# Two transformer blocks on one core: the order of the last projection's heads, the row slots and a run of table copies

## The reference, cut to what matters

```python
def peer_layer(h, w_q, sub_keys, u_tab, v_tab):
    ...
    q = (hf @ w_q).reshape(T, PEER_HEADS, 2, PEER_DQ // 2)
    s = jnp.einsum('thpd,hpnd->thpn', q, sub_keys)
    sc, idx = lax.top_k(s, PEER_TOPK)
    ...
    top_sc, pos = lax.top_k(cand, PEER_TOPK)
    eidx = jnp.take_along_axis(cidx, pos, axis=-1)
    gate = jax.nn.softmax(top_sc.astype(jnp.float32), axis=-1).astype(h.dtype)
    ...
        act = jax.nn.gelu(jnp.einsum('thkd,td->thk', u_tab[eb], hb), approximate=False)
        return jnp.einsum('thk,thkd->td', gb * act, v_tab[eb])
...
        u2 = rms_norm_2(h, norm2_g[l]) * (1 + sc2) + sh2
        h = h + g2 * peer_layer(u2, peer_wq[l], peer_keys[l], peer_u[l], peer_v[l])
    return rms_norm_2(h, final_g)
```

## Time and profile before

| what | value |
|---|---|
| median of 3 runs | 1728.81 us (1722.48 to 1732.06) |
| profiled execution: time | 1722.41 us |
| profiled execution: span of the core | 1720.6 us |
| TensorE busy | 1523.9 us (89%) |
| VectorE busy | 1026.8 us (60%) |
| ScalarE busy | 533.0 us (31%) |
| GpSimd busy | 558.6 us (32%) |
| mean TensorE clock granted | 0.95 of full |
| chain that ended last | PE 67%, DMA 20%, DVE 8% |
| row fetches | 256, 268.45 MB |

### The profile page before, as it was taken

The page is one execution under the profiler, slowest core; times in us unless marked ns, Lnnn a source line. Parts: engine busy times, 40 slices in busy tenths (PEclk is TensorE's granted clock), DMA queues, the critical chain, the costliest instruction groups (busy, mean ns, idle before and its releaser), DMA issues.

```text
span 1720.6 us, 22658 instructions
## 1 busy us (share of the span) xinstructions
PE 1523.9 (89%) x8228; PEld 1161.9 (68%) x8228; DVE 1026.8 (60%) x2104; ACT 533.0 (31%) x1069; POOL 558.6 (32%) x361
## 2 busy tenths in 40 slices
PE   6999989999699999999999989878787778777876
PEld 6999988678599999998889988433333333333332
DVE  5554355655233325998984744657676766758555
ACT  4443353352244335443116421312121212121111
POOL 3555353000134432001001402454454544444540
PEclk9999999899799998999999999898999998899998
DMA  6666699819979997998975836799999999999994
GB/s 264 241 227 247 245 350 378 279 46 342 386 284 371 370 366 284 365 371 308 346 255 196 342 105 275 307 428 426 428 426 427 427 427 427 426 427 427 427 427 194
DMA packets 98724, 571.87 MB, mean 332 GB/s; under 512 B 10960, under 2 KB 11088, under 8 KB 48976
## 3 DMA queue, kind: packets, MB, share of 16 engines
q1 hardware_dynamic: 60624, 297.89, 47.3%
q0 software_dynamic: 36864, 268.45, 37.1%
q10 hardware_dynamic: 1152, 4.43, 0.7%
HBM read 569.68 MB, written 135.27 MB: 410 GB/s over the span
## 4 chain that ended last, share of the span: by engine, by line
PE 67%; DMA 20%; DVE 8%; issue 2%; ACT 2%; SPq 2%; POOL 0%; ACTq 0%; DVEq 0%; POOLq 0%
DMA arena<-pairs,eidx 16%; PE ps L2125 11%; PE ps L1612 9%; PE ps L1614 9%; PE ps L1613 9%; PE ps L1957 5%; PE ps L2090 3%; PE ps L1663 2%; PE ps L1665 2%; PE ps L1664 2%; DMA ring<-pairs,eidx 2%; PE ps L1974 2%; DVE arena L1530 2%; DMA ring<-in_stream 1%; PE ps L1627 1%
## 5 line engine op out<-in xcount | busy, mean ns | idle before, releaser
L2125 PE MATMUL ps<-arena 128*128 128x512 f32 x720 | 346.3, 636 | 85.3 <-ACT arena L997 85.2
L634 POOL TENSOR_TENSOR w_lo<-ring,w_hi 128x1024 fp32r<-128x1024 f32 x82 | 216.2, 2638 | 446.7 <-DVE w_lo L1059 366.3
L2125 PEld LDWEIGHTS ps<-arena 128*128 128x128 f32 x720 | 144.2, 204 | 285.5 <-issue 174.1
L1612 PE MATMUL ps<-u_hi,w_hi 128*128 128x256 f32 (+1 forms) x1056 | 305.1, 289 | 9.9 <-DVE u_lo L1028 9.9
L1614 PE MATMUL ps<-u_hi,w_lo 128*128 128x256 f32 (+1 forms) x1056 | 303.3, 287 | 0.0
L1613 PE MATMUL ps<-u_lo,w_hi 128*128 128x256 f32 (+1 forms) x1056 | 302.9, 287 | 0.0
L1530 DVE CUSTOM_DVE_ANT_0 arena<-arena 128x1024 f32<-128x1024 f32 x180 | 218.9, 1223 | 138.7 <-DMA arena<-pairs,eidx 138.7
L664 POOL DMA_INDIRECT arena<-pairs,eidx x180 | 213.4, 1185 | 254.8 <-PE ps L2125 202.4
L681 ACT ACTIVATE w_hi<-ring 128x1024 fp32r<-128x1024 f32 x188 | 197.9, 1056 | 191.5 <-PE ps L1665 77.5
L1612 PEld LDWEIGHTS ps<-u_hi,w_hi 128*128 128x128 f32 x1056 | 201.9, 191 | 12.6 <-issue 10.7
L1614 PEld LDWEIGHTS ps<-u_hi,w_lo 128*128 128x128 f32 x1056 | 202.2, 192 | 0.0
(11 more groups left out here) (301 smaller groups left out, 2461.0 us busy)
## 6 DMA issues: line engine op xcount, KB each, us to landing
ring<-in_stream SPq DMA_DIRECT2D x130, 1024.0 KB, 7.0
pairs<-in_peer_u SPq DMA_DIRECT2D x128, 512.0 KB, 7.6
pairs<-in_peer_v SPq DMA_DIRECT2D x128, 512.0 KB, 8.8
arena<-in_ada SPq DMA_DIRECT2D x32, 768.0 KB, 6.3
arena<-pairs,eidx POOLq DMA_INDIRECT x180, 17.9
ring<-pairs,eidx POOLq DMA_INDIRECT x76, 17.3
h<-in_x_t SPq DMA_DIRECT2D x1, 1088.0 KB, 7.8
arena<-in_keys ACTq DMA_DIRECT2D x1, 1024.0 KB, 7.0
```

What stands on the lines that cost most here:

```text
L634: pool.tensor_tensor(lo[:, half, :], ring[:, slot, e * HALF:(e + 1) * HALF], hi[:, half, :], ALU.subtract).then_inc(used if e else lo_done, 1)
L1612: pe.matmul(dst, hi[:, half, block], x[0][:, b, 0:w], start=(b == 0), stop=False)
L2125: mm = pe.matmul(ps[:, Y_BANKS[j // TOPK] + half, :], diag[:, n % DIAGS, :], slot_of(n)[:, D + half * 512:D + half * 512 + 512], start=(hd ...
```

## The change

It has four parts. (1) The ten blocks behind the `ada` loads move in front of them (BEFORE_ADA = 24). (2) The first head is projected, scored and copied tile by tile, in products of 128 columns. Only heads 1 to 4 follow it; head 5 is done on TensorE and ScalarE behind group 1, head 6 behind group 8, head 7 behind group 12, followed by the gain. (3) There are again 13 row slots, now eleven in the arena (the room of `h_tok` and `final_g`) and two in the ring, those of the pieces of heads 4 and 5. Rows 0 to 10 go to the arena, row 11 to the ring when head 4 is projected, rows 12 to 19 to the slots of rows 0 to 7, row 20 to the ring when head 5 is projected; then the order repeats with period 13. The sums of the two tiles lie in PSUM banks 0 to 3. (4) The last four rows are groups of one. Of the last tile's work, gain, residual and squares of tile 0 go between the dots of rows 248 to 250, and both scalings and stores come at the end. h is transposed to PSUM banks 4 to 7 between groups 44 to 50 and read from there; `final_g` is loaded by SP once the last head is chosen.

```diff
 ADA_W = 6 * D // ADA_Q
-ARENA_SLOTS = 9
-SLOTS = ARENA_SLOTS + RING
+ARENA_SLOTS = 11
+SLOTS = ARENA_SLOTS + 2
 HEAD_ROWS = TT * TOPK
 ROWS = HEADS * HEAD_ROWS
 GROUP = 4
+GROUPS = [slice(n, n + GROUP) for n in range(0, ROWS - GROUP, GROUP)] + [slice(n, n + 1) for n in range(ROWS - GROUP, ROWS)]
+RING_HEADS = [4, 5]
+LATER_HEADS = {1: 5, 8: 6, 12: 7}
 DIAGS = 8
 N_BLOCKS = NKEYS * NKEYS // P
 W_IN_BLOCKS = 7
 ADA_BLOCKS = 1
-BEFORE_ADA = 14
-AFTER_ADA = 10
-FINAL_STEPS = 5
+BEFORE_ADA = 24
...
 
         NORM_COLS = [slice(0, T), slice(0, T), xc, xc, xc]
 
-        Y_BANKS = [2, 4]
+        Y_BANKS = [0, 2]
+        RING_SLOTS = [(BASE["wq"] + hd) % RING for hd in RING_HEADS]
+        SLOT_AT = list(range(ARENA_SLOTS)) + [ARENA_SLOTS] + list(range(8)) + [ARENA_SLOTS + 1]
+        while len(SLOT_AT) < ROWS:
+            SLOT_AT.append(SLOT_AT[-SLOTS])
+        TURN = [SLOT_AT[:n].count(SLOT_AT[n]) for n in range(ROWS)]
 
         def slot_of(n):
 
-            at = n % SLOTS
-            return rows[:, at, :] if at < ARENA_SLOTS else ring[:, at - ARENA_SLOTS, :]
+            at = SLOT_AT[n]
+            return rows[:, at, :] if at < ARENA_SLOTS else ring[:, RING_SLOTS[at - ARENA_SLOTS], :]
 
         def landing(n):
-            return row_in[n % SLOTS], n // SLOTS * 16 + 16
+            return row_in[SLOT_AT[n]], TURN[n] * 16 + 16
+
+        def held_before(n):
+            return max(i for i in range(n) if SLOT_AT[i] == SLOT_AT[n])
+
+        def q_bank(hd):
+            return 6 if hd >= 6 else hd % 2 * 2
+
+        def q_pieces(hd):
+            return 2 * hd + 2 * TT
+
+        def score_pieces(hd):
+            return hd + TT
 
 
...
                     for n in range(ADA_BLOCKS):
                         pair_up(kt * (ADA_Q * ADA_BLOCKS) + (at + q * ADA_BLOCKS + n))
             at += (KT // 2 - 2) * ADA_Q * ADA_BLOCKS
-            for n in range(AFTER_ADA):
-                pair_up(at + n)
-            at += AFTER_ADA
             for part, end, each in (("ffn2", "z_gate", 1), ("z_gate", "w_b", 2), ("w_b", "wq", 1)):
                 load_pieces(BASE[part], BASE[end], at, each)
                 at += (BASE[end] - BASE[part]) * each
             assert at == N_BLOCKS
             load_pieces(BASE["wq"], N_PIECES)
+            sp.wait_ge(idx_done, score_pieces(HEADS - 1))
+            sp.dma_start(final_g, a["final_g"].rearrange("(o d) -> o d", o=1).broadcast_to([P, D])).then_inc(final_in, 16)
             for t in range(TT):
-                sp.wait_ge(fin_step, (t + 1) * FINAL_STEPS)
+                sp.wait_ge(fin_step, 3 * TT + 2 * (t + 1))
                 sp.dma_start(out[0, t * P:(t + 1) * P, :], acc[:, t, :]).then_inc(out_done, 16)
             sp.wait_ge(out_done, 16 * TT)
 
...
+                    pool.wait_ge(idx_done, score_pieces(hd) if hd else 1)
                 elif hd == 0 and j == TOPK:
                     pool.wait_ge(idx_done, TT)
-                if n == ARENA_SLOTS:
-                    pool.wait_ge(q_mm, 2 * HEADS)
-                if n >= SLOTS:
-                    pool.wait_ge(row_summed, n - SLOTS + 1)
+                if TURN[n]:
+                    pool.wait_ge(row_summed, held_before(n) + 1)
+                elif SLOT_AT[n] >= ARENA_SLOTS:
+                    pool.wait_ge(q_mm, q_pieces(RING_HEADS[SLOT_AT[n] - ARENA_SLOTS]))
                 pool.indirect_dma_start(slot_of(n), None, pairs, bass.IndirectOffsetOnAxis(ap=eidx[:, n:n + 1], axis=0)
                                         ).then_inc(landing(n)[0], 16)
 
...
+            def first_head(t):
+
+                c = slice(t * P, (t + 1) * P)
                 for e in range(2):
-                    act.wait_ge(q_mm, hd * 2 + e + 1)
+                    act.wait_ge(q_mm, t * 2 + e + 1)
+                    act.activation(qh[:, 0, e, c], ps[:, e, c], ACT.Copy).then_inc(q_ev, 1)
+                tok_copy(2 * t)
+                act.wait_ge(sc_mm, t + 1)
+                act.activation(scores[:, 0, t].rearrange("p e n -> p (e n)"), ps[:, 4, t * SEQ:(t + 1) * SEQ], ACT.Copy
+                               ).then_inc(sc_ev, 1)
+                tok_copy(2 * t + 1)
...
+            for t in range(TT):
+                first_head(t)
+            for hd in range(1, min(LATER_HEADS.values())):
+                head(hd)
+                if hd == 2:
+                    gate_exp(0)
...
+                if g in LATER_HEADS:
+                    head(LATER_HEADS[g])
+                if g == max(LATER_HEADS):
+                    act.wait_ge(gain_mm, 1)
+                    for half in range(2):
+                        act.activation(y_gain[:, half * 512:half * 512 + 512], ps[:, 6 + half, :], ACT.Copy).then_inc(tok_ev, 1)
+            mean_root(0)
             mean_root(1)
...
-            def finish(t):
+                    dve.wait_ge(diag_made, group.stop - HEAD_ROWS)
+                dve.tensor_tensor(wts[:, j:end], dots[:, j:end],
+                                  gate[:, hd % 2].rearrange("p t k -> p (t k)")[:, j:end], ALU.mult).then_inc(w_done, 1)
+
+            def gained(t):
 
                 dve.wait_ge(row_summed, ROWS - (TT - 1 - t) * TOPK)
+                if t == 0:
+                    dve.wait_ge(tok_ev, 6)
                 summed = ps[:, Y_BANKS[t]:Y_BANKS[t] + 2, :].rearrange("p b d -> p (b d)")
-                if t == 0:
-                    dve.wait_ge(tok_ev, 10)
-                    dve.wait_ge(final_in, 16)
                 then(dve.tensor_tensor(acc[:, t, :], summed, y_gain, ALU.mult), fin_step)
-                then(dve.tensor_tensor(acc[:, t, :], acc[:, t, :], h_tok[:, t, :], ALU.add), fin_step)
+
+            def added(t):
+
+                dve.wait_ge(tok_mm, 2 * TT + 2 * t + 2)
+                kept = ps[:, 4 + 2 * t:6 + 2 * t, :].rearrange("p b d -> p (b d)")
+                then(dve.tensor_tensor(acc[:, t, :], acc[:, t, :], kept, ALU.add), fin_step)
+
+            def squared(t):
 
                 then(dve.tensor_tensor_reduce(hf[:, t, :], acc[:, t, :], acc[:, t, :], 1.0, 0.0, ALU.mult, ALU.add,
                                               fin[:, 2 * t:2 * t + 1]), fin_step)
+
+            def scaled(t):
+
...
+                for n in range(group.start, group.stop):
+                    dot(n)
+                    if n == group.start and g:
                         weights(g - 1)
+                    if n == ROWS - 8:
+                        gained(0)
+                    if n == ROWS - 7:
+                        added(0)
+                    if n == ROWS - 6:
+                        squared(0)
...
+            weights(len(GROUPS) - 1)
+            gained(1)
+            added(1)
+            squared(1)
+            scaled(0)
+            scaled(1)
...
+            def residual_turn(n):
+
+                t, half = n // 2, n % 2
+                if n == 0:
+                    pe.wait_ge(sc_ev, score_pieces(HEADS - 1))
+                    pe.wait_ge(tok_ev, 6)
+                for i in range(4):
+                    mm = pe.transpose(ps[:, 4 + n, i * P:(i + 1) * P], h[:, half * 4 + i, X0 + t * P:X0 + (t + 1) * P], ident)
+                mm.then_inc(tok_mm, 1)
...
+            def first_head(t):
+
+                slot = BASE["wq"] % RING
+                c = slice(t * P, (t + 1) * P)
+                if t == 0:
+                    pe.wait_ge(landed[slot], BASE["wq"] // RING * 16 + 16)
+                for e in range(2):
+                    for b in range(KT):
+                        if t == 0 and e == 0:
+                            pe.wait_ge(u_done, 4 * KT + b + 1)
+                        mm = pe.matmul(ps[:, e, c], blk(slot, e * KT + b), u[:, b, c], start=(b == 0), stop=(b == KT - 1))
+                    mm.then_inc(q_mm, 1)
+                if t == TT - 1:
+                    pe.wait_ge(q_mm, q_pieces(0))
+                    pe.sem_inc(used, 1)
+                tok_turn(2 * t)
+                pe.wait_ge(q_ev, 2 * t + 2)
+                scores_with(0, t).then_inc(sc_mm, 1)
+                tok_turn(2 * t + 1)
...
+                if hd < HEADS - RING:
+                    pe.wait_ge(q_mm, q_pieces(hd))
                     pe.sem_inc(used, 1)
...
+            for t in range(TT):
+                first_head(t)
+            for hd in range(1, min(LATER_HEADS.values())):
+                head(hd)
+            for g in range(len(GROUPS)):
+                if g - 1 in LATER_HEADS:
+                    head(LATER_HEADS[g - 1])
+                    if g - 1 == max(LATER_HEADS):
+                        gain_turn()
+                weigh_rows(g)
+                if len(GROUPS) - 23 <= g < len(GROUPS) - 15 and g % 2 == 0:
+                    residual_turn((g - (len(GROUPS) - 23)) // 2)
```

## The result

The changed kernel takes 1699.71 us (median of 4 runs, 1696.46 to 1700.80), the kernel before 1728.38 (median of 4, 1722.48 to 1732.06): ratio 0.9836, 95% interval 0.981 to 0.986, 28.7 us less. Its profiled execution took 1700.73 us, span 1698.9.

What follows compares the result with a forecast made beforehand. The prediction took the row stage to end when its copies end, with TensorE's early head projections the bound from 1060 to 1095 us. Gains 17.5 + 13 + 0 = 30.5 from 1728.8 gave 1698.3 us, range 1714 down to 1683.

Steps and rivals of the forecast that it cites:

- The copies, 17.5: Second feed-forward's norm: moving ten blocks of pair copies lets its weight pieces go earlier, gaining 17.5 us (bounds 12 and 20).
- The cost of the copies in the attention: First two ada loads go out 32 us later but stay hidden: cost 0, at most a few us.
- the sum by the page: Same norm: without the pause TensorE's clock may stay up, so the gain would be some 20 us, not 17.5.
- The row stream, 13: Fetch of the 256 expert rows: earlier start gives 20.5, late heads lose 7; ends 13 us earlier (bounds 5 and 22).
- the late end: Row 25 lands at 1107 to 1111 instead of 1131.6; taking the later time gives 20.5 us earlier.
- 15 us of lateness: Heads 6 and 7 behind groups 8 and 12: 7.8 and 10.9 late, some 3.5 made up, together about 15 us.
- The place of the pause (row 65): Sign in the row stream: a pause of 4 to 7 us around row 65, none if the late heads cost nothing.
- Rival 1: Late heads eat the row stream's gain, leaving only 3 to 5 us; time 1707 us; chance 0.18.
- rival 2: Late heads cost nothing because the row slots absorb all; time 1691 us; chance 0.12.
- The end, 0: After the last row lands: TensorE ends 8.9 us later, tile scaling adds 1; together 0 (2 worse to 4 better).
- The copies running into the attention (3): Second feed-forward does not start earlier: something such as these copies takes the gain back; time 1716 us; chance 0.07.
- TensorE as the bound of the rows (4): Row stream: groups restarting at the low clock cost more than 9.82 us each, so the kernel is slower; chance 0.03.

Runs made afterwards that it cites:

- twelve single rows: The changed kernel with one-row groups for the last twelve rows in place of four: 1690.47 us, ratio 0.9762 to the kernel before.
- four profiles of unchanged order: Two more profiles of the kernel before (1727.11, 1737.63 us) and two of the changed kernel with the copies put back (1720.34, 1714.47 us).
- `after`: The changed kernel as first measured, with all four parts, against the kernel before: 1699.71 us, ratio 0.9836; its profiled execution took 1700.73 us.

## Why the prediction was right

**The copies, 17.5: right, with some luck in the number.** The mean gain at the norm in front of the expert layer is 17.0 (1014.3 - 997.3), and 19.8 in the time of the kernel with only the copies moved. The mechanism is as told: the norm of the second feed-forward follows the projection without a pause in all eight profiles with moved copies, and its sum is ready 68.3 us behind the third ada load in each, where the six others need 85.6 to 88.7. They are held by the landing of two pieces in a loaded queue, which varies; the profile of before had the shortest. So at this point the copies give 19.2 in the mean and not 17.5, and some 2 of it are lost on the way to the expert layer, at TensorE's clock, which the sum had not foreseen: the two nearly cancel. The first piece was issued at the predicted place (426.62 less the 4.0 of the attention is 422.6). The cost of the copies in the attention was taken as 0, and is 0 as far as the profiles can tell. Without the pause the norm's 16 matmuls take 3.69 at a granted clock of 1.00, where they took 5.58 at 0.66. The rule of the Trainium skill that was weighed beside this term (TensorE: Matmul & The Clock Gate, "What's actually happening": an idle array is throttled until activity releases it) agrees with that. But the norm's sum was ready at 448.3 to 448.6 in the four profiles whose attention was not late, 448.0 predicted, and not 2.5 earlier as the sum by the page had it.

**The row stream, 13: right, with two steps that cancel.** Row 0 is issued 22.8 us behind the norm where 25.6 were, the 3 predicted (at 1021.49 and not near 1012, since the norm itself was late in this pair). A head takes 8.59 us by the two rows named for it, not 8.55, which changes the sum by 0.1. From the norm, row 25's dot comes 22.7 us earlier (124.5 to 101.8, means over four and seven profiles), where 20.5 was taken as the late end. From row 25 to row 255 the changed kernel takes 580.0 and the kernel before 570.3: 9.7 lost to heads 6 and 7, where the prediction had 7 from an estimate of 15 us of lateness. The lateness was 10.0 + 12.95 less 5.5 that three groups made up, so 17.4; the heads took 19.8 and 22.75 for the 17.6 and 20.7 worked out. With the heads at 12 and 20 the loss is 3.2 (573.5), and with only one head behind group 1 it is 0.9. So their place is shown to matter; two things change with it, the choosing part in the groups behind group 8 and the distance between the heads (four groups or eight), and no run parts them. The place of the pause (row 65) was right. Rival 1 had the loss too large, and rival 2 (no cost) is refuted by the windows and by the moved heads.

**The end, 0: right, 0.8 gained** (0.6 in the first pair): TensorE ends 8.5 after the last dot starts, 8.9 predicted: its last eight rows start 5.5 before that dot and take 14.0 (the prediction's own terms, 14.4 less 7.6, give 6.8; the 2.1 up to its 8.9 stand in none of its rows). The span ends 9.8 behind TensorE where 8.7 were, the 1 us more of the tiles' last work. That the backlog comes from group 62, not from the last four rows, is shown by the twelve single rows.

**Rivals 3 and 4.** The copies running into the attention (3) was what the first pair of profiles seemed to say, and four profiles of unchanged order took it back. TensorE as the bound of the rows (4) does not happen: from 1208 on the stream never pauses (426 GB/s).

What stays open: why TensorE's clock is low in some executions between 300 and 350 us, at the sums and around 800 us. The last two are where 2.1 us go between the norm's sum of the second feed-forward (19.1 earlier in the mean, 469.4 to 450.3) and the norm of the expert layer (17.0).

## What to carry to other kernels

Work with slack in an in-order queue belongs in front of a stretch in which the queue is empty, not in front of the load that the next stage waits for; look for it wherever the transfer share is 0 before a stage and full at its start. When side work is put into a stream that lives on a few slots, count the lateness of each insertion against what the next groups can make up, and leave room behind each: groups with nothing else to do, and enough of them before the next insertion. And cut every profile at fixed marks: one pair of profiles here misstated one part by 9 us, while the rows part of the changed kernel lay within 3.2 us of its mean in each of seven profiles.

## What the runs showed of the hardware

The same instructions, before anything had changed in them, ran at either of the two levels of TensorE's clock (1.2 and 2.4 GHz) from one execution to the next: 24 matmuls at 338 us in 3.56 us at a granted clock of 1.00, or in 6.18 at 0.50. The 48 one-column matmuls took 5.42 to 8.20, behind a stretch without a pause as well as behind one. In the profile of `after` TensorE was busy for 3.68 of the 3.70 us ahead of them at a clock of 1.00, and then for all of their 7.70 us at a mean of 0.68: the clock fell while the engine was not idle. With what else varies ahead of it, the start of the expert layer moved by 15.0 us over three profiles of the kernel before (1006.6 to 1021.6), while its rows part took 695.0 to 695.2. In the kernels with the changed row order and moved copies it moved by 10.6, and the rows by 6.2 (heads at 8 and 12); why the rows vary more there was not tested.
